# Two of eight weight chunk pairs of nine gate/up groups computed as 2x2 block products in seven multiplications, with block sums made on VectorE

## The reference

```
def swiglu(x, w_gate, w_up, w_down):
    return (jax.nn.silu(x @ w_gate) * (x @ w_up)) @ w_down

x = x + 0.5 * swiglu(rms_norm(x, ffn1_norm[l]), ffn1_w_gate[l], ffn1_w_up[l], ffn1_w_down[l])
...
x = x + 0.5 * swiglu(rms_norm(x, ffn2_norm[l]), ffn2_w_gate[l], ffn2_w_up[l], ffn2_w_down[l])
```

## Time and profile before

| what | value |
|---|---|
| median of three runs | 1830.43 us (1830.24 to 1830.84) |
| the profiled execution, its own time | 1831.22 us |
| its span in the trace | 1828.9 us |
| busy TensorE | 1817.0 us, 99% |
| busy VectorE | 1016.0 us, 56% |
| busy ScalarE | 829.6 us, 45% |

### The profile page before, as it was taken

The page is one execution under the profiler, slowest core; times in us unless marked ns, Lnnn a source line. Parts: engine busy times, 40 slices in busy tenths (PEclk is TensorE's granted clock), DMA queues, the critical chain, the costliest instruction groups (busy, mean ns, idle before and its releaser), DMA issues.

```text
span 1828.9 us, 22464 instructions
## 1 busy us (share of the span) xinstructions
PE 1817.0 (99%) x8105; PEld 1500.3 (82%) x8105; DVE 1016.0 (56%) x1237; ACT 829.6 (45%) x986; POOL 31.4 (2%) x36
## 2 busy tenths in 40 slices
PE   9999999999999999999999999999999999999998
PEld 7888888888888888888888888888888888888886
DVE  6555555555545555557657766555555555554554
ACT  6444444444444444545455455444444444443443
POOL 0000000000000000000000000000000000000000
PEclk9999999999999999999999999999999999999999
DMA  7666666667666656765665566767776767655554
GB/s 256 205 203 203 205 206 206 203 203 205 205 205 207 203 195 202 225 188 181 189 206 175 186 209 206 205 205 206 205 203 203 205 202 207 208 199 195 194 195 139
DMA packets 207563, 368.03 MB, mean 201 GB/s; under 512 B 19600, under 2 KB 37648, under 8 KB 207376
## 3 DMA queue, kind: packets, MB, share of 16 engines
q1 hardware_dynamic: 206784, 365.51, 64.9%
q0 software_dynamic: 144, 1.05, 0.2%
q10 hardware_dynamic: 576, 0.69, 0.1%
HBM read 347.25 MB, written 2.10 MB: 191 GB/s over the span
## 4 chain that ended last, share of the span: by engine, by line
PE 99%; DMA 1%; SPq 0%; ACT 0%; DVE 0%; issue 0%; DVEq 0%; ACTq 0%
PE bank L382 33%; PE bank L384 32%; PE bank L383 32%; DMA x<-in_x_dram 1%; PE bank L508 0%; PE bank L525 0%; PE bank L420 0%; PE bank L516 0%; PE bank L439 0%; PE bank L533 0%; SPq L263 0%; ACT x L629 0%; DVE yT_lo L1005 0%; SPq L314 0%; ACT w_hi L596 0%
## 5 line engine op out<-in xcount | busy, mean ns | idle before, releaser
L814 DVE TENSOR_TENSOR w_lo<-raw,w_hi 128x1024 fp32r<-128x1024 f32 x655 | 806.3, 1232 | 775.3 <-ACT w_hi L596 774.8
L596 ACT ACTIVATE w_hi<-raw 128x1024 fp32r<-128x1024 f32 x655 | 693.6, 1060 | 910.9 <-PE bank L384 905.8
L382 PE MATMUL bank<-w_hi,xT_hi 128*128 128x512 f32 x1788 | 699.3, 391 | 0.0
L384 PE MATMUL bank<-w_hi,xT_lo 128*128 128x512 f32 x1788 | 696.1, 389 | 0.0
L383 PE MATMUL bank<-w_lo,xT_hi 128*128 128x512 f32 x1788 | 695.8, 389 | 0.0
L382 PEld LDWEIGHTS bank<-w_hi,xT_hi 128*128 128x128 f32 x1788 | 335.7, 188 | 71.5 <-issue 2.7
L384 PEld LDWEIGHTS bank<-w_hi,xT_lo 128*128 128x128 f32 x1788 | 335.7, 188 | 70.1
L383 PEld LDWEIGHTS bank<-w_lo,xT_hi 128*128 128x128 f32 x1788 | 335.8, 188 | 68.5
L382 PE MATMUL bank<-w_hi,hT_hi 128*128 128x512 f32 x704 | 273.9, 389 | 0.0
L383 PE MATMUL bank<-w_lo,hT_hi 128*128 128x512 f32 x704 | 273.9, 389 | 0.0
L384 PE MATMUL bank<-w_hi,hT_lo 128*128 128x512 f32 x704 | 273.9, 389 | 0.0
(11 more groups left out here) (115 smaller groups left out, 417.8 us busy)
## 6 DMA issues: line engine op xcount, KB each, us to landing
raw<-in_ffn_w_up_dram SPq DMA_DIRECT2D x176, 512.0 KB, 3.9
raw<-in_ffn_w_down_dram SPq DMA_DIRECT2D x176, 512.0 KB, 3.6
raw<-in_ffn_w_gate_dram SPq DMA_DIRECT2D x175, 512.0 KB, 3.7
raw<-in_w_in_dram SPq DMA_DIRECT2D x96, 512.0 KB, 4.2
raw<-in_w_out_dram SPq DMA_DIRECT2D x32, 512.0 KB, 4.1
turn_in<-gate SPq DMA_DIRECT2D x448, 32.0 KB, 2.6
x<-in_x_dram SPq DMA_DIRECT2D x3, 512.0 KB, 9.7
out_dram<-x SPq DMA_DIRECT2D x6, 256.0 KB, 2.7
```

What stands on the lines that cost most here:

```text
L382: pe.matmul(acc, hi[:, kt, ts], w_hi[slot][:, kk], start=(k == 0 and kk == 0), stop=False)
L384: mm = pe.matmul(acc, lo[:, kt, ts], w_hi[slot][:, kk], start=False, stop=(k == chunks - 1 and kk == KC - 1))
L596: act.activation(w_hi[slot][:], raw[slot][:], ACT.Copy).then_inc(hi_ready, 1)
L814: dve.tensor_tensor(w_lo[slot][:], raw[slot][:], w_hi[slot][:].bitcast(F32), ALU.subtract)\
```

## The change

In each feed-forward, groups 1 to 9 are worked in another way; group 0 and group 10 stay as they were. In a changed group the gate chunk k and the up chunk k follow each other (k = 0 to 7). For k = 2 and k = 5 (`SEVEN`) the pair is one 2 x 2 block product: row tiles by input blocks on one side, input blocks by gate and up on the other. Instead of eight block products TensorE makes seven, by Winograd's form. What TensorE multiplies in a changed group is a list of 20 **forms**, numbered 0 to 19 here; each takes a slot of the `w_hi`/`w_lo` ring as a chunk did:

- 12 plain chunks (forms 0 to 3, 8 to 11, 16 to 19), gate and up in turn, 12 matmuls each
- for k = 2 the forms 4 (raw gate), 5 (raw up, changed in place), 6 (two block sums), 7 (one block sum, half a chunk), with 6, 6, 6 and 3 matmuls; for k = 5 the forms 12 to 15, likewise

The block sums of weights are four additions of DVE for each pair (`sum_weights`), made before the low part of form 4 or 12, and they need both raw chunks of the pair. Three of the products go to PSUM banks 4 to 7 (M1, M5, M6, M7), gathered over both pairs. Behind the low part of form 20 (form 0 of the next group) DVE combines them (four additions that read a bank) in `gate` and `turn_in`, after ACT has copied M1; at the group's end DVE adds banks 0 and 1 to that (two), ACT takes the silu from SBUF, and DVE adds banks 2 and 3 (two) and multiplies (two scalar_tensor_tensor, now from SBUF). The sums of the activations are made once in each feed-forward, in group 0 (`form_stationary`, `split_forms`). Forms 18 and 19, the last of a group, end banks 0/1 and 2/3; form 0 of the next group needs the first pair drained and form 1 the second.

The core of the diff:

```diff
+SEVEN = (2, 5)
+FORMS, FORM_OF = [], {}
+for _k in range(CD):
+    for _u in range(2):
+        FORM_OF[2 * _k + _u] = len(FORMS)
+        FORMS.append(("raw", 2 * _k + _u))
+    if _k in SEVEN:
+        FORMS += [("sum", 0), ("sum", 1)]
+NF = len(FORMS)
+SUMMED = [FORM_OF[2 * k] for k in SEVEN]
...
+            def seven_group(f, base, wg, wu, c):
+                for r in range(2 * CD):
+                    k, u = divmod(r, 2)
+                    sp.wait_ge(lo_ready, base + (FORM_OF[r - RING] if r >= RING else r - RING) + 1)
+                    src = (wg, wu)[u][0].rearrange("(k p) n -> p k n", p=P)[:, KC * k:KC * k + KC, bass.ds(c * W, W)]
+                    sp.dma_start(raw[r % RING][:], src).then_inc(raw_loaded[r % RING], 16)
+                    if CD <= r < CD + QUADS:
+                        move_hidden(f, c, r - CD)
+            def sevens(f, ch, wg, wu):
+                with sp.Fori(1, GROUPS - 1) as c:
+                    seven_group(f, c * NF + (ch + 2 * CD - NF), wg, wu, c)
+                gate_up(f, ch + SURPLUS, wg, wu, GROUPS - 1)
...
+            def product(acc, hi, lo, slot, b, start, stop):
+                pe.matmul(acc, hi, w_hi[slot][:, b], start=start, stop=False)
+                pe.matmul(acc, hi, w_lo[slot][:, b], start=False, stop=False)
+                return pe.matmul(acc, lo, w_hi[slot][:, b], start=False, stop=stop)
+            def seven_group(f, base, pair):
+                def x_of(t, kt):
+                    ts = slice(t * P, (t + 1) * P)
+                    return xT_hi[:, kt, ts], xT_lo[:, kt, ts]
+                for n, (kind, r) in enumerate(FORMS):
+                    slot = n % RING
+                    pe.wait_ge(lo_ready, base + n + 1)
+                    if n < 2:
+                        banks_free(pair, n)
+                    ks = [k for k in SEVEN if 0 <= n - FORM_OF[2 * k] < 4]
+                    if not ks:
+                        k, u = divmod(r, 2)
+                        for t in range(TT):
+                            for b in range(KC):
+                                mm = product(bank[2 * u + t][:], *x_of(t, KC * k + b), slot, b, n < 2 and b == 0,
+                                             n >= NF - 2 and b == KC - 1)
+                            if n >= NF - 2 and t == 0:
+                                mm.then_inc(upper_done, 1)
+                    else:
+                        s = SEVEN.index(ks[0])
+                        a, b = KC * ks[0], KC * ks[0] + 1
+                        s1, s2, s3, s4 = [(seven_x[:, s, 0, i], seven_x[:, s, 1, i]) for i in range(4)]
+                        first, last = s == 0, s == len(SEVEN) - 1
+                        if n == FORM_OF[2 * ks[0]]:
+                            product(M1, *x_of(0, a), slot, 0, first, last)
+                            mm = product(bank[0][:], *x_of(0, b), slot, 1, False, False)
+                        elif n == FORM_OF[2 * ks[0]] + 1:
+                            if first:
+                                pe.wait_ge(forms_ready, len(SEVEN) * (f + 1))
+                            product(M7, *s3, slot, 0, first, last)
+                            mm = product(bank[2][:], *s4, slot, 1, False, False)
+                        elif r == 0:
+                            product(M5, *s1, slot, 0, first, last)
+                            mm = product(M6, *s2, slot, 1, first, last)
+                        else:
+                            mm = product(bank[1][:], *x_of(1, b), slot, 0, False, False)
+                    mm.then_inc(chunk_used, 1)
...
+            def seven_high(base, raws, n, s0):
+                act.wait_ge(chunk_used, base + n - RING + 1)
+                kind, r = FORMS[n] if n < NF else ("raw", 2 * CD + n - NF)
+                if kind == "raw":
+                    act.wait_ge(raw_loaded[r % RING], ring_count(raws + r, r % RING))
+                    if n - 1 in SUMMED:
+                        act.wait_ge(sums_ready, s0 + SUMMED.index(n - 1) + 1)
+                    act.activation(w_hi[n % RING][:], raw[r % RING][:], ACT.Copy).then_inc(hi_ready, 1)
+                elif r == 0:
+                    act.activation(w_hi[n % RING][:], seven_sums[:, 0:2], ACT.Copy).then_inc(hi_ready, 1)
+                else:
+                    act.activation(w_hi[n % RING][:, 0], seven_sums[:, 2], ACT.Copy).then_inc(hi_ready, 1)
+            def seven_group(f, base, raws, pair, hid, c):
+                s0 = c * len(SEVEN) + len(SEVEN) * (f * (GROUPS - 2) - 1)
+                for n in range(NF):
+                    seven_high(base, raws, n + RING, s0)
+                    if n == 8:
+                        split_hidden(hid, c - 1)
+                    if n == SUMMED[-1] + RING:
+                        act.activation(seven_m1, M1, ACT.Copy).then_inc(m1_copied, 1)
+                    if n == NF - 2:
+                        for t in range(TT):
+                            act.wait_ge(drained[0], pair * TT + t + 1)
+                            act.activation(gate[:, t], gate[:, t], ACT.Silu, scale=rstd[:, t:t + 1]).then_inc(silu_done, 1)
...
+            def seven_low(base, n):
+                dve.wait_ge(hi_ready, base + n + 1)
+                slot = n % RING
+                kind, r = FORMS[n] if n < NF else ("raw", 2 * CD + n - NF)
+                if kind == "raw":
+                    full, hi, lo = raw[r % RING][:], w_hi[slot][:], w_lo[slot][:]
+                elif r == 0:
+                    full, hi, lo = seven_sums[:, 0:2], w_hi[slot][:], w_lo[slot][:]
+                else:
+                    full, hi, lo = seven_sums[:, 2], w_hi[slot][:, 0], w_lo[slot][:, 0]
+                dve.tensor_tensor(lo, full, hi.bitcast(F32), ALU.subtract).then_inc(lo_ready, 1)
+            def sum_weights(first_raw, k):
+                r1, r2 = 2 * k % RING, (2 * k + 1) % RING
+                dve.wait_ge(raw_loaded[r1], ring_count(first_raw + 2 * k, r1))
+                dve.wait_ge(raw_loaded[r2], ring_count(first_raw + 2 * k + 1, r2))
+                u1, u2, u4 = [seven_sums[:, i] for i in range(3)]
+                link(dve.tensor_tensor(u1, raw[r1][:, 0], raw[r2][:, 0], ALU.add))
+                dve.tensor_tensor(raw[r2][:, 0], raw[r2][:, 0], raw[r2][:, 1], ALU.add)
+                link(dve.tensor_tensor(u2, u1, raw[r2][:, 1], ALU.add))
+                dve.tensor_tensor(u4, u2, raw[r1][:, 1], ALU.add).then_inc(sums_ready, 1)
+            def seven_group(f, base, raws, pair, hid, c):
+                s0 = c * TT + TT * (f * (GROUPS - 2) - 1)
+                for n in range(NF):
+                    if n + RING in SUMMED:
+                        sum_weights(raws, SEVEN[SUMMED.index(n + RING)])
+                    if n == 0:
+                        dve.wait_ge(drained[1], pair * TT)
+                        turn_quads(turn_in, hid_turned)
+                    if n == NF - 2:
+                        for t in range(TT):
+                            unit_done(base + NF - 1, pair, 0, t)
+                            if t == 0:
+                                g = dve.tensor_tensor(gate[:, 0], bank[0][:], seven_m1, ALU.add)
+                            else:
+                                g = dve.tensor_tensor(gate[:, 1], bank[1][:], gate[:, 1], ALU.subtract)
+                            g.then_inc(drained[0], 1)
+                    if n == NF - 1:
+                        for t in range(TT):
+                            unit_done(base + NF, pair, 1, t)
+                            link(dve.tensor_tensor(turn_in[:, t], bank[2 + t][:], turn_in[:, t], (ALU.subtract, ALU.add)[t]))
+                            dve.wait_ge(silu_done, s0 + t + 1)
+                            dve.scalar_tensor_tensor(out=turn_in[:, t], in0=turn_in[:, t], scalar=rstd[:, t:t + 1],
+                                                     in1=gate[:, t], op0=ALU.mult, op1=ALU.mult).then_inc(drained[1], 1)
+                    seven_low(base, n + RING)
+                    if n == 9:
+                        split_hidden(hid, c - 1)
+                    if n == SUMMED[-1] + RING:
+                        dve.wait_ge(hid_lo, hid + c)
+                        dve.wait_ge(m1_copied, c + f * (GROUPS - 2))
+                        link(dve.tensor_tensor(gate[:, 0], M6, seven_m1, ALU.add))
+                        dve.tensor_tensor(turn_in[:, 0], M5, gate[:, 0], ALU.add)
+                        link(dve.tensor_tensor(gate[:, 1], M7, gate[:, 0], ALU.add))
+                        link(dve.tensor_tensor(turn_in[:, 1], M5, gate[:, 1], ALU.add))
+            def sevens(f, ch, pr, hid):
+                more = NF - 2 * CD
+                with dve.Fori(1, GROUPS - 1) as c:
+                    steps.enter(c - 1, 2 * len(SEVEN) + 3 + TT)
+                    seven_group(f, c * NF + (ch - more), c * (2 * CD) + (ch - f * SURPLUS), c + pr, hid, c)
+                steps.leave(GROUPS - 2)
+                gate_up(ch + SURPLUS, pr, hid, GROUPS - 1)
+            def form_stationary(f, s):
+                kt = KC * SEVEN[s]
```

(15 more changed lines are left out.)

78 lines of the change are left out of this document (54 added, 24 removed).

## The result

The changed kernel takes 1835.25 us (median; 1834.1 to 1838.3) against 1830.52 for the kernel before: ratio 1.0026, interval 1.0018 to 1.0035. The forecast was 1829.0 and no measurable change; the kernel is 4.7 us slower, more than the 3.7 that the prediction gave as the least that a measurement can tell. The profiled run took 1835.75 us, 4.5 more than that of before.

The account below looks back on a forecast made before the run. TensorE bounds the kernel, but a 43.6 us loop through DVE, SP and loads would hold changed groups: 12.24 us saved less 11.5 of waits per feed-forward, twice, net 1.4 us, giving 1829.0 us, range 1815 to 1843.

Parts of the forecast that it names:

- The term L: Period of a changed group, set by a loop through DVE, SP and loads: 43.6 us, above TensorE's 42.16.
- What bounds the kernel now: Whole kernel: TensorE, busy 1817.0 of 1828.9 us; only fewer matmuls without new waits save time.
- what is removed: Changed groups: 2 x 3 matmuls less each, 42.16 us instead of 43.52; eighteen save 24.5 us without waits.
- The prices on DVE: New 128x512 additions: 0.685 us each, pitch 0.60, linked 0.72; DVE takes 36.4 of 42.16 us a group.
- Rival 3: DVE's additions from banks cost 0.06 to 0.07 us more: loop 44.1, 1837 us; slower side altogether 0.31.
- Rival 4: DVE's instructions don't overlap, each costs its full duration: loop 45.0, 1851 us; chance 0.04.
- The loop that decides: Changed groups: a chain through DVE, SP's moves, loads and ACT, without TensorE, sums to 43.51, with registers 43.6 us.
- the late drain: Banks 2 and 3 at group end: drain has one chunk's cover, 2.72 us, not eight; four instructions take 2.8.
- Each 0.1 us of the loop is 1.6 us: Steepness over 16 groups: change is -24.5 + 16 (L - 42.16) us.
- What costs nothing: Group 0's activation sums, at most 4.3 us of DVE, hide in 5.6 us slack; ACT has room; same bytes loaded.
- The sum: Two feed-forwards: each saves 12.24 us and pays 11.5 in waits; net 1.4 us, giving 1829.0.
- rival 2: No measurable change: loop between 43.46 and 43.92, time 1829, own range 1826.5 to 1834; chance 0.35.

Follow-up runs that it names:

- e8: Changed kernel with pairs 2 and 4, moves on GpSimd's queue, form 22's low part behind the last multiplies, ten extra SP increments: 1807.31 us (0.9875).
- e11: Kernel of e8 without its ten SP increments and with 93 do-nothing increments in TensorE's program: 1805.44 us (0.9863).
- e14: Changed kernel with the low part of form 22 moved behind the last two multiplies, pairs 2 and 5, moves on SP: 1841.85 us (1.0062).
- e6: Kernel of e3 with the low part of form 22 moved behind the last multiplies: 1809.3 us (0.9884).
- e12: Changed kernel with pairs 3 and 5, form 22's low part behind last multiplies, DVE wait before second sums, 93 TensorE increments, moves on SP: 1811.22 us.
- e15: Changed kernel without the four M additions L1085 to L1088, output not the block's: 1820.33 us (0.9944).
- e3: Changed kernel with the moves of groups 1 to 9 on GpSimd's queue instead of SP's, hidden block split three forms later: 1826.7 us (0.9980).
- e10: Changed kernel with 93 do-nothing semaphore increments in TensorE's program, behind chunks of the first down product: 1840.0 us (1.0054).
- e9: The changed kernel itself, unedited, run again on a later occasion: 1840.13 us (1.0053).

## Why the prediction was wrong

Two steps failed. The term L, the loop, was sized 43.6 us and measured 43.86; and the sum had no term for stages that weren't edited, where the w_out stage took 1.7 us more. Together they turned -1.4 into +4.4. Step by step:

1. **What bounds the kernel now; what is removed**: right. 108 matmuls, and at TensorE's own pace a group takes 42.16 us to the last digit (e8, e11).
2. **The prices on DVE**: right within 0.01 us for the additions (0.685 taken; 0.68 to 0.69 from SBUF and from banks; linked pitch 0.72 = 269.53 - 268.81). Rival 3's mechanism is refuted, and with it the rule in the Trainium skill, "VectorE: DVE Perf Modes", section "The TRN2 errata", for this instruction: L1085 reads a bank in 0.68 us, L1051 SBUF in 0.69. Rival 4 is refuted by the pitches of 0.61 (269.53 to 270.14).
3. **The loop that decides**: the mechanism was right, shown by e14 (moving the drain alone is worth 1 us), e6 and e12 (with the loop shortened too, the groups fall to 42.2 to 42.5) and e15. Two things beside it were not seen. The way over TensorE's forms 1 to 4 to load 10 is as long: the 0.2 us that form 8's low part was given to spare were not there, which costs some 0.02. And the late drain alone would hold a group at about 43.4 to 43.6 (e3). The size failed, in the sum of the term L. Forecast 43.6, measured 43.86, the mean of both feed-forwards. In the group above 0.11 were on SP (3.11 from load to load instead of 3.07, all of it at load 10, 0.28 behind the moves where 0.16 had been read), 0.02 ahead of load 8, 0.24 between the sums of pair 5 and the first load, 0.10 in the M additions and 0.10 in the drains; against these stand 0.14 and 0.08 less for the landings, 0.04 less in the low parts between, and the 0.1 allowed for registers. What was mis-sized: a low part to the load that waits for it is 1.40 us (261.63 to 263.03; form 16 is the first of the four in that row), not 1.26; ScalarE adds 0.1 before form 13; and a register behind a link costs 0.09 (0.81 instead of 0.72: 271.67 - 270.86, 275.95 - 275.14), not 0.05. "Each 0.1 us of the loop is 1.6 us": 0.26 is 4.2 of the 6.2 us between 1829.0 and 1835.25.
4. **TensorE waits 1.44 us in each of 16 groups at form 1, by L1077**: right in place and number. At form 1 the start is 1.24 us late (1.1 of it idle), with 0.1 in the next starts, and 0.2 at form 14, as foreseen.
5. **What costs nothing**: right for group 0, where TensorE's one wait for DVE stands at the very start (12.43 us) and none behind the sums of activations, which begin at 38.59. What failed is a term that wasn't named: the change also moved the place of TensorE's instruction fetches in the rest of its program, and two of them fell on rows of SP that stand ahead of data for ScalarE. +1.7 us of the +4.5, shown by e10 beside e9 (1.6 us back in the stage for 93 instructions that do nothing, though not in the medians) and e11 (1.7 back in the stage and 1.9 in the time, against e8).
6. **The sum**: -1.4 forecast; +2.7 from the groups and +1.7 from the w_out stage make +4.4, measured +4.5 (profiled), +4.7 (medians). The loop of 43.86 lies inside the interval of rival 2 (43.46 to 43.92), for which no measurable change was forecast: it was the 1.7 us of the w_out stage that carried the first measurement past 3.7. So it is luck which side of that line the first measurement took. Rival 3's side came true by other means: a longer loop by registers and SP, and on the later occasions, as far as the landings show, by these (1840.1, 1842.8), which I had named beside it at 1842.

What stays open: why landings take 0.2 to 0.3 us longer on some occasions (the chip, or something in its state), and why SP's issue stops when a packet of q8 passes; neither was tried further.
